# Expert rows placed at a rotating slot, and the weights W1 and W3 laid out as 16 neighbouring rows per partition

## The reference, cut to what matters

```python
xt = h.reshape(n, d)                      # 512 tokens x 2048, after an RMS norm with gain norm_ffn
...                                       # a group of 8 experts, then 2 experts in it, gives expert_id, gate
counts = jnp.bincount(eid, length=MOE_EXPERTS)
...                                       # tokens are sorted by expert and padded to blocks
def block_ffn(args):
    xb, e = args
    return (jax.nn.silu(xb @ w1[e]) * (xb @ w3[e])) @ w2[e]     # w1, w3: 2048 x 384; w2: 384 x 2048
...
y = jnp.zeros((n, d), h.dtype).at[tok_s].add(ypad[dest] * wgt_s[:, None])
```

## Time and profile before

| | us |
|---|---|
| median of 3 runs | 2582.9 (2581.25 to 2582.98) |
| the profiled execution, its own time | 2581.16 |
| its span, first to last instruction | 2579.0 |
| PE busy (x13063 instructions) | 2353.1 (91%) |
| DVE busy | 831.3 (32%) |
| ACT busy | 351.5 (14%) |
| POOL busy | 395.1 (15%) |
| DMA, mean over the span | 277 GB/s, 714.63 MB |

### The profile page before, as it was taken

One profiled execution on the slowest core, in us unless ns is written; L12 is line 12 of the kernel. 1 busy time (PEld: TensorE's weight loads), 2 busy tenths in 40 slices (PEclk: granted clock), 3 DMA queues, 4 the chain that ended last, 5 costly groups with the idle time before them and its releaser, 6 DMA issues.

```text
span 2579.0 us, 32836 instructions
## 1 busy us (share of the span) xinstructions
PE 2353.1 (91%) x13063; PEld 1229.0 (48%) x13063; DVE 831.3 (32%) x1318; ACT 351.5 (14%) x595; POOL 395.1 (15%) x574
## 2 busy tenths in 40 slices
PE   8999999999899999999998888888888888888887
PEld 5433444445588875644444434443444344434443
DVE  5499928334644431411111111111111111111113
ACT  2100022101422222100100000000000000000002
POOL 3466300000132200011110110011001110110100
PEclk9999999999999999999999999999999999999999
DMA  6221211221122145699999999999999999999995
GB/s 187 82 65 33 67 64 54 66 65 60 48 85 75 51 145 225 261 415 427 426 426 425 425 426 426 424 420 423 417 422 418 417 412 417 405 424 400 420 394 242
DMA packets 142980, 714.63 MB, mean 277 GB/s; under 512 B 33752, under 2 KB 92956, under 8 KB 99260
## 3 DMA queue, kind: packets, MB, share of 16 engines
q1 hardware_dynamic: 115416, 691.09, 65.8%
q0 software_dynamic: 18432, 16.83, 1.9%
q10 hardware_dynamic: 9060, 5.68, 0.7%
HBM read 718.11 MB, written 45.61 MB: 296 GB/s over the span
## 4 chain that ended last, share of the span: by engine, by line
PE 47%; DMA 39%; DVE 10%; issue 2%; ACT 1%; POOL 0%; SPq 0%; ACTq 0%; DVEq 0%; POOLq 0%
DMA big<-in_moe_w 38%; PE ps L2228 14%; PE ps L2568 12%; PE ps L2282 5%; DVE big L1218 4%; PE ps L2597 4%; PE ps L2452 2%; PE ps L2372 1%; DVE big L1350 1%; PE ps L2582 1%; DVE big L1349 1%; PE ps L2357 1%; DMA big<-y_rows 1%; PE ps L2554 1%; PE ps L2038 1%
## 5 line engine op out<-in xcount | busy, mean ns | idle before, releaser
L2568 PE MATMUL ps<-big 128*64 128x384 f32 x4096 | 710.5, 503 | 126.9 <-DMA big<-in_moe_w 114.4
L2568 PEld LDWEIGHTS ps<-big 128*64 128x64 f32 x4096 | 301.5, 141 | 542.4 <-issue 401.0
L2228 PE MATMUL ps<-big 128*128 128x512 f32 (+2 forms) x1216 | 532.1, 597 | 1.6 <-ACT big L918 1.6
L2597 PE MATMUL ps<-big 128*64 128x512 f32 x1536 | 385.4, 656 | 51.8 <-DVE big L1978 51.8
L2228 PEld LDWEIGHTS ps<-big 128*128 128x128 f32 (+2 forms) x1216 | 227.9, 189 | 296.5 <-issue 294.4
L1974 DVE TENSOR_SCALAR big<-ps,scal 128x384 f32<-128x384 f32 x64 | 39.6, 618 | 739.7 <-PE ps L2568 739.7
L2597 PEld LDWEIGHTS ps<-big 128*64 128x64 f32 x1536 | 114.1, 149 | 275.5 <-issue 214.9
L1983 DVE SCALAR_TENSOR_TENSOR big<-ps,scal,big 128x512 f32<-128x512 f32 x128 | 90.2, 747 | 392.1 <-PE ps L2597 392.1
L2282 PE MATMUL ps<-big 128*128 128x256 f32 x768 | 184.2, 390 | 3.0 <-DMA big<-in_w_out 1.9
L2282 PEld LDWEIGHTS ps<-big 128*128 128x128 f32 x768 | 141.9, 191 | 28.2 <-issue 4.8
L820 POOL COPY scal<-slots 128x3 f32 (+1 forms) x64 | 11.9, 186 | 924.6 <-DVE big L1983 906.1
(11 more groups left out here) (402 smaller groups left out, 1694.7 us busy)
## 6 DMA issues: line engine op xcount, KB each, us to landing
big<-in_moe_w SPq DMA_DIRECT2D x192, 3072.0 KB, 40.1
big<-in_w_in SPq DMA_DIRECT2D x18, 2048.0 KB, 8.2
big<-in_w_out SPq DMA_DIRECT2D x8, 1024.0 KB, 5.9
big<-y_rows SPq DMA_DIRECT2D x8, 1024.0 KB, 14.1
big<-in_x SPq DMA_DIRECT2D x4, 1024.0 KB, 8.4
big<-in_w_out SPq DMA_DIRECT2D x8, 512.0 KB, 7.0
big<-in_x SPq DMA_DIRECT2D x16, 256.0 KB, 2.8
big<-in_w_out SPq DMA_DIRECT2D x1, 4096.0 KB, 14.2
```

The costliest lines, as they stand in the source:

```text
L2228: last = nc.tensor.matmul(ps[n % 2][0:wd, :], ring[s % 2][:, k, c:c + wd], hT[:, k, :], start=(k == 0), stop=(k == NC - 1))
L2568: last = nc.tensor.matmul(ps[2 + w][B * g:B * g + B, 0:FF], xT[k][:, j, B * g:B * g + B], W13[k][w][:, NJ * g + j, :], start=(j == 0), sto ...
L2597: last = nc.tensor.matmul(ps[5 + q][B * g:B * g + B, :], hid[k][:, m, :], W2[k][:, m, 512 * n:512 * n + 512], start=(m == 0), stop=(m == F ...
```

## The change

1. A row's slot in block b is its old slot plus 9 b, modulo 64 (`ROT = 9`). Block 0 is unchanged, block 1 begins at slot 9, block 8 at slot 8 (72 modulo 64). On VectorE that is a turn of `s8`, four small operations where there was one. For the short way of blocks 0 and 1 three small iotas on GpSimd make `frank`, which takes the place of a list of ranks.
2. W1, W3 and the gain are read as 16 neighbouring rows per partition: partition p holds input features 16p to 16p + 15, one run of 24576 bytes. Features 0 to 1023, half 0, lie then in partitions 0 to 63, and half 1 in partitions 64 to 127.
3. So `turn` no longer transposes over all 128 partitions. A half row stays in its half of the partitions and is turned in a 64x64 tile on the diagonal of the array: 16 columns times 2 halves, 32 small transposes for the 8 large ones. Half 0 uses the transpose instruction, half 1 a matmul with the identity. The two halves of a step write different PSUM banks (h = z ^ g).
4. `turn` waits once for both halves of `xT`, and tells VectorE after the last of its steps, for both banks at the same time. `columns` waits for both, and its two operations have the same 512 columns as before. `up` has the same number and sizes of matmuls.

```diff
--- before.py
+++ after.py
@@ -251,7 +251,7 @@
         W2 = [wide(i, 12).rearrange("p (c n) -> p c n", c=FC) for i in (36, 48)]
         xg = [wide(78 + 2 * k, 2)[:, 0:DG] for k in range(2)]
         yb = [wide(74 + 2 * k, 2)[:, 0:DG] for k in range(2)]
-        xT = [wide(84 + 2 * k, 2)[:, 0:NJ * P].rearrange("p (c t) -> p c t", c=NJ) for k in range(2)]
+        xT = [wide(84 + 2 * k, 2)[:, 0:NC * B].rearrange("p (c t) -> p c t", c=NC) for k in range(2)]
         uv = [wide(88 + 2 * k, 2)[:, 0:2 * FF].rearrange("p (w f) -> p w f", w=2) for k in range(2)]
         hid = [big[:, 92 + k, 0:FC * B].rearrange("p (c t) -> p c t", c=FC) for k in range(2)]
         sil = [big[:, 92 + k, 256:256 + FC * B] for k in range(2)]
@@ -273,6 +273,9 @@
 
         tokv = rt[:, 5700:5708]
         gcol = rt[:, 5720:5721]
+
+        ROT = 9
+        frank = rt[:, 5440:5440 + 2 * B].rearrange("p (e t) -> p e t", e=2)
         blockt = wide(82)[:, 0:2 * NTT * NBLK].rearrange("p (q b) -> p q b", b=NBLK)
         fastv = big[:, 77, :].rearrange("p (q t) -> p q t", t=B)
         slot1 = rt[:, 4928:4928 + 2 * NTT * B].rearrange("p (q t) -> p q t", t=B)
@@ -572,11 +575,10 @@
             sp.wait_ge(rwy_ok, WT)
             for i in range(2, NTT):
                 sp.dma_start(x2[i][:, 0:1792], x2d[P * i:P * (i + 1), 0:1792]).then_inc(x2b_in, 16)
-            sp.dma_start(gffn[:].rearrange("p (g c) -> p g c", g=GR), I["norm_ffn"][0].rearrange("(g p c) -> p g c", g=GR, c=NJ)).then_inc(gain_in, 16)
+            sp.dma_start(gffn[:], I["norm_ffn"][0].rearrange("(p c) -> p c", c=NC)).then_inc(gain_in, 16)
 
             def load13(e, k, w):
-                sp.dma_start(W13[k][w].rearrange("p (g c) f -> p g c f", g=GR),
-                             I[("moe_w1", "moe_w3")[w]][0][e].rearrange("e (g p c) f -> p (e g) c f", g=GR, c=NJ)).then_inc((w1_in, w3_in)[w][k], 16)
+                sp.dma_start(W13[k][w], I[("moe_w1", "moe_w3")[w]][0][e].rearrange("e (p c) f -> p (e c) f", c=NC)).then_inc((w1_in, w3_in)[w][k], 16)
 
             def load2(e, k):
                 sp.dma_start(W2[k], I["moe_w2"][0][e].rearrange("e (p c) n -> p (e c) n", c=FC)).then_inc(w2_in[k], 16)
@@ -784,6 +786,8 @@
             fl = dict(allow_small_or_imprecise_dtypes=True)
             nc.gpsimd.iota(rv(0, 8), pattern=[[1, 8]], base=0, channel_multiplier=0, **fl)
             nc.gpsimd.iota(rv(1, NBLK), pattern=[[1, NBLK]], base=0, channel_multiplier=0, **fl)
+            for e, a, n, base in ((0, 0, B, 1), (1, ROT, B - ROT, 1), (1, 0, ROT, B - ROT + 1)):
+                nc.gpsimd.iota(frank[:, e, a:a + n], pattern=[[1, n]], base=base, channel_multiplier=0, **fl)
             for a, n, base in ((0, NE - 2, 0), (NE - 2, NBLK - NE, NE), (LAST, 2, NE - 2)):
                 nc.gpsimd.iota(rv(2, NBLK)[:, a:a + n], pattern=[[1, n]], base=base, channel_multiplier=0, **fl)
             nc.gpsimd.iota(rv(3, 1), pattern=[[0, 1]], base=-NE, channel_multiplier=1, **fl)
@@ -1854,8 +1858,8 @@
             v.do(nc.vector.scalar_tensor_tensor(out=fr.rearrange("p (i e) -> p i e", e=2), in0=rank[:, :, 0:2], scalar=1.0,
                                                 in1=rv(12, NTT, NE)[:, :, 0:2], op0=ADD, op1=MUL))
             v.settle()
-            v.tell(nc.vector.tensor_tensor(fastv, rv(1, NBLK)[:, 1:B + 1].unsqueeze(1).to_broadcast([P, 2 * NTT, B]),
-                                           fr.unsqueeze(2).to_broadcast([P, 2 * NTT, B]), ALU.is_equal), tabf_ok, 2)
+            v.tell(nc.vector.tensor_tensor(fastv.rearrange("p (i e) t -> p i e t", e=2), frank.unsqueeze(1).to_broadcast([P, NTT, 2, B]),
+                                           fr.rearrange("p (i e) -> p i e", e=2).unsqueeze(3).to_broadcast([P, NTT, 2, B]), ALU.is_equal), tabf_ok, 2)
             nb, pend, pst = (rv(7, 320)[:, 32 + 64 * j:96 + 64 * j] for j in range(3))
             sc(nb, src[:, NTT * NE:NTT * NE + NE], 1.0, -0.5 * B - 0.5, ALU.max, ADD)
             v.settle()
@@ -1878,6 +1882,7 @@
             dif, fits = rv(8, 320)[:, 128:128 + NE], rv(12, NTT, NE)
             both = rt[:, 3200:3840].rearrange("p (k n) -> p k n", k=2)[:, :, 0:NTT * NE]
             dest8, b8, s8 = (rt[:, 5648 + 8 * j:5656 + 8 * j] for j in range(3))
+            turn8, wrap8 = rt[:, 5736:5744], rt[:, 5744:5752]
             v.do(nc.vector.scalar_tensor_tensor(out=dif, in0=rv(1, NBLK)[:, 0:NE], scalar=float(B), in1=pst, op0=MUL, op1=SUB))
             op(place, rank, pst.unsqueeze(1).to_broadcast([P, NTT, NE]), ADD)
             v.settle()
@@ -1894,7 +1899,13 @@
             v.settle()
             sc(b8, b8, MAGIC, MAGIC, ADD, SUB)
             v.settle()
-            v.do(nc.vector.scalar_tensor_tensor(out=s8, in0=b8, scalar=-float(B), in1=dest8, op0=MUL, op1=ADD))
+            v.do(nc.vector.scalar_tensor_tensor(out=turn8, in0=b8, scalar=float(ROT), in1=dest8, op0=MUL, op1=ADD))
+            v.settle()
+            sc(wrap8, turn8, 1.0 / B, 0.5 / B - 0.5, MUL, ADD)
+            v.settle()
+            sc(wrap8, wrap8, MAGIC, MAGIC, ADD, SUB)
+            v.settle()
+            v.do(nc.vector.scalar_tensor_tensor(out=s8, in0=wrap8, scalar=-float(B), in1=turn8, op0=MUL, op1=ADD))
             slotv = slots[:].rearrange("p (b v) -> p b v", v=3)
             op(block1, rv(2, NBLK).unsqueeze(1).to_broadcast([P, 2 * NTT, NBLK]), b8.unsqueeze(2).to_broadcast([P, 2 * NTT, NBLK]), ALU.is_equal)
             v.settle()
@@ -1931,15 +1942,13 @@
             sc(picks, ptok, wrap[:, NBLK - 1:NBLK], None, ALU.is_equal)
             v.settle()
             dve.wait_ge(gain_in, 16)
-            g4 = gffn[:].rearrange("p (g j) -> p j g", g=GR)
 
             def columns(r, k):
+                dve.wait_ge(xtp_ok, 4 * r + 2 * k + 2)
                 for h in range(2):
-                    cs = slice(NJ // 2 * h, NJ // 2 * h + NJ // 2)
-                    dve.wait_ge(xtp_ok, 4 * r + 2 * k + 1 + h)
-                    nc.vector.tensor_tensor(xT[k][:, cs, :].rearrange("p c (g t) -> p c g t", g=GR),
-                                            ps[h][:, 0:NJ * P // 2].rearrange("p (c g t) -> p c g t", c=NJ // 2, g=GR),
-                                            g4[:, cs].unsqueeze(3).to_broadcast([P, NJ // 2, GR, B]), MUL).then_inc(xT_ok, 1)
+                    cs = slice(NJ * h, NJ * h + NJ)
+                    nc.vector.tensor_tensor(xT[k][:, cs, :], ps[h][:].rearrange("p (c t) -> p c t", c=NJ),
+                                            gffn[:, cs].unsqueeze(2).to_broadcast([P, NJ, B]), MUL).then_inc(xT_ok, 1)
 
             columns(0, 0)
             op(blockv[:, :, 0, :], block1, gate[:].rearrange("p k i -> p (k i)").unsqueeze(2).to_broadcast([P, 2 * NTT, NBLK]), MUL)
@@ -2543,16 +2552,22 @@
                 pe.wait_ge(xg_in[k], 16 * (r + 1))
                 if first:
                     pe.wait_ge(xz_ok, k + 1)
-                for h in range(2):
-                    if not (first and k == 0):
-
-                        pe.wait_ge(xT_ok, 4 * r + 2 * k - 1 + h)
-
-                    pe.sem_inc(passed, 1)
-                    for j in range(NJ // 2):
-                        c = NJ // 2 * h + j
-                        last = nc.tensor.transpose(ps[h][:, P * j:P * j + P], xg[k].rearrange("t (p c) -> t c p", c=NJ)[:, c], ident[:])
-                    last.then_inc(xtp_ok, 1)
+                if not (first and k == 0):
+                    pe.wait_ge(xT_ok, 4 * r + 2 * k)
+                pe.sem_inc(passed, 1)
+
+                for z in range(2):
+                    for j in range(NJ):
+                        for g in range(GR):
+                            h = z ^ g
+                            rows = slice(B * g, B * g + B)
+                            x_, o_ = xg[k].rearrange("t (p c) -> t c p", c=NC)[rows, NJ * h + j], ps[h][rows, B * j:B * j + B]
+                            if g:
+                                last = nc.tensor.matmul(o_, x_, ident[rows, rows], start=True, stop=True)
+                            else:
+                                last = nc.tensor.transpose(o_, x_, ident[rows, rows])
+                            if z and j == NJ - 1:
+                                last.then_inc(xtp_ok, 1)
 
             def up(r, k, first):
                 pe.wait_ge(xT_ok, 4 * r + 2 * k + 2)
@@ -2565,7 +2580,7 @@
                         pe.wait_ge((u_ok, v_ok)[w], 2 * r + k)
                     for j in range(NJ):
                         for g in range(GR):
-                            last = nc.tensor.matmul(ps[2 + w][B * g:B * g + B, 0:FF], xT[k][:, j, B * g:B * g + B], W13[k][w][:, NJ * g + j, :],
+                            last = nc.tensor.matmul(ps[2 + w][B * g:B * g + B, 0:FF], xT[k][:, NJ * g + j, :], W13[k][w][:, NJ * g + j, :],
                                                     start=(j == 0), stop=(j == NJ - 1))
                     last.then_inc(up_ok, 1)
```

## The result

The changed kernel takes 3082.8 us (median of 4 runs, 3082.07 to 3084.64), the kernel before 2582.7 (2581.25 to 2582.98): ratio 1.1939, 95% interval 1.1918 to 1.196. It is 500 us slower; the forecast was 2546, and the sign was wrong.

A forecast was written before the change was run, and what follows sets the result against it. DMA engines streaming weights were taken as the bound, the slowest pair setting the end: 2581.2 - 34 (rotation) - 8 (layout) + 2.6 (routing, first turns) + 3 (lower clock) = 2545, with the median's offset 2546; range 2532 to 2582.

The forecast's parts named there:

- the sign: Whole kernel: the change was to make it faster, chance 0.84, with same at 0.04 and slower at 0.12.
- What bounds the kernel: Expert stage: full DMA engines streaming weights set the pace, the slowest pair sets the end, TensorE close behind.
- the stair: End of the weight stream: DMA share falls 0.42, 0.32, 0.25, 0.13, put down to uneven gathers and scatters.
- The rotation: Gathers and scatters: even rows over engines save 20 us at the end and 14 before, together 34.
- The layout of the weights: Weight loads: 256 fewer packets a block at 8 ns each save 8 us, from nothing to 14.
- I take 2.1: `turn`: its 32 small steps were to take 2.1 us, adding 1.0 us a block for TensorE.
- The nearest rows: `turn`: 64x64 diagonal pairs at 33 and 43 ns an instruction, giving 2.1 to 2.75 us for 16 pairs.
- The upper bound: `turn`: if nothing of the halves overlaps, 48 loads of 135 ns each make 6.5 us.
- Rival 2: `turn`: alternating transposes and matmuls don't overlap, 6.5 us each, total 2800; decides from 3.0 us on; chance 0.12.
- The cover: TensorE's wait for weights: 0.3 us a block to hide the longer `turn`, holding until it costs about 2.4.
- The even stream: Expert stage: evenly loaded DMA engines make a block last 22.4 us, where TensorE needs 22.1.

The follow-up runs named there:

- e3: The kernel before with only the rotation of the slots added, layout of weights and `turn` as before: 2544.6 us, ratio 0.9863.
- g4: The kernel before with the rotation of the slots alone, run once more: 2545.5 us, ratio 0.9864.
- f2: e3 with W1 and W3 also loaded as runs of 24576 bytes per partition, not computing the reference: 2535.5 us, ratio 0.9824.
- e2: The changed kernel with the loop over halves outermost, 16 transposes then 32 matmul instructions, one switch in a `turn`: 2787.4 us, ratio 1.0798.
- f4: The changed kernel with transposes and matmuls in groups of four, 7 switches in a `turn`: 2860.3 us (one run).
- g3: The changed kernel with half 1 left out and half 0 alternating transpose and matmul in one 64x64 tile, not computing the reference: 2786.5 us (one run).
- f1: e1 with each small tile reading 64 neighbouring columns instead of columns 64 bytes apart, not computing the reference: 2538.4 us, ratio 0.9833.
- g1: The changed kernel, still alternating, with each small tile reading 64 neighbouring columns, not computing the reference: 3022.5 us (one run).
- f3: The kernel before with all eight 128x128 transposes of a `turn` done as matmuls with the identity: 2637.4 us (one run).
- e1: The changed kernel with both halves turned by matmuls with the identity, no transpose instructions in `turn`: 2641.3 us, ratio 1.0237.
- g2: The changed kernel's rotation and layout, with `turn` using only transposes of 128 rows by 64 columns, computing the reference: 2538.1 us, ratio 0.9837.

## Why the prediction was wrong

- What bounds the kernel, and the stair: right. DMA set the pace, and the engines were uneven. One reading was off: the earlier trace rows count 63 waits, not blocks; in the trace they lie in 47 of the 64 blocks, two in some and none in the first eleven. The sums use the total and stand. The rotation was put at 34 us less 0.6, bounds 29 to 39; alone it gives 36 (e3, g4).
- The layout of the weights: right. 8 us forecast, 9 measured (f2).
- `turn`: the step that failed. "I take 2.1" was 10.0 us. Four things were in it. The nearest rows, lines 2357 and 2372, are matmuls alone; between a matmul and a transpose there is a switch of 0.14 us, 31 times, 4.2 us (e2, f4, g3). They also read neighbouring columns, which I did not look at: columns 64 bytes apart made a matmul instruction in one tile 115 ns, where twice the 32 of f1's pairs is about 65, 1.6 us in a `turn` (from g1's step it is 2.1, with the transposes). The two halves were to overlap, and did not: 16 + 32 instructions of about 66 ns one after another are 3.2 us and not 2.1. And the lower clock adds 1.1 us (9.96 against 16 x 0.556).
- The upper bound failed too: 6.5 us, each load by itself. The earlier trace rows hold a safer one, the mean length of a matmul, 220 ns: 48 x 220 = 10.6 us, above the 8.9 measured at the full clock and the 10.0 with the lower one. That is an estimate seen afterwards: it takes each instruction to wait for the whole of the one before, which no run shows.
- Rival 2 was the right mechanism, with a threshold that the runs agree with (3.0 us; f3 and e1, at 3.9 and 3.7, are slower than before; no run has a `turn` between 2.4 and 3.7) and too small a price: 2800. With 10.0 us its own formula gives 21.1 + 8.9 = 30.0 a block and 3017; measured are 30.7 and 3083. The rest is clock (`gather_hidden` 2.8 for 2.05) and the delayed start. The clock has a part in the 500 us that no rival counted: 1.1 us in `turn` and 0.7 in `gather_hidden`, about 110 us over 62 blocks. It stood at 0.12. The rule that speaks for it was weighed beside it, and that no row had the mix should have made it one of two equal cases.
- The cover: right as a limit. The even stream was to leave TensorE a block of 22.4 us (in f2 it is 22.3), and once `turn` cost more, the gains of rotation and layout could not show, since the DMA engines were no longer the bound (share 0.77 in 1600:2500, against 1.00).

## What to carry to other kernels

When a diff mixes two kinds of TensorE instruction in small tiles and no row shows the mix, price it from above by the full length of the instructions (here 10.6 us for a `turn` of 10.0), not by their loads (6.5), and see whether the cover holds at that price. Keep the kinds in groups, or use one kind; read the stride of the operands on both sides of an analogy before taking its duration. The stair in the DMA share at the end of the stream came from uneven engines here, and moving the partitions that sparse transfers hit was worth more (36 us) than larger transfers (9 us).

## What was not expected of the hardware

- A switch between a transpose and a matmul in 64x64 tiles costs about 0.14 us, in the same tile as in another; at 128x128 it costs nothing that could be measured (2.42 us against 2.45 added up).
- Float32 matmuls whose stationary operand is strided are slower: 64 columns 64 bytes apart take 58 ns an instruction in pairs, neighbouring ones 32 (e1, f1). For 128 columns 32 bytes apart it is 244 ns (f3); no run has the same matmuls with neighbouring columns. Transposes of 128 rows by 64 columns follow each other in 0.11 us both with columns 64 bytes apart (g2) and with neighbouring ones (line 2329 of the kernel before).
- In g2 the granted clock is 1.00 over the whole stage, where it was 0.95 before and 0.97 in e3, although `up` still waits up to 2.1 us for weights. g2 has no pause of 0.8 us before `down`; that this is why the clock stays up was not tested.
